# Attention steps placed between the products of the plain projections, in one hybrid trunk layer

## What is computed

```python
z = x @ w_in
# A: 16 heads of 64, 4 kv heads, window 128: a block of 128 queries sees its own and the previous 128 keys
s = einsum("bnqhgd,bnkhd->bnhgqk", q, k) * (dh ** -0.5) + bias
m = maximum(s.max(-1), sink)
p = exp(s - m)
A = einsum("bnhgqk,bnkhd->bnqhgd", p / (p.sum(-1) + exp(sink - m)), v)
# B: RWKV-7 time mixing, a scan over the tokens
mix = (sigmoid(gate_attn) * (A @ w_branch_attn) + sigmoid(gate_rwkv) * (B @ w_branch_rwkv)) @ w_out
h = layer_norm(alpha * x + mix)
# PEER: for each token and 8 heads, the 16 best of 128^2 experts
y = layer_norm(alpha * h + sum(gate * gelu(u[e] . h) * v[e]))
```

## Time and profile before

| | us |
|---|---|
| median of three runs | 4366.49 |
| lowest, highest | 4365.15, 4375.88 |
| the profiled execution | 4375.91 |
| its span on the core | 4374.1 |
| PE busy | 3791.0 (87%) |
| PE weight load busy (beside PE) | 2533.3 (58%) |
| DVE busy | 3035.9 (69%) |
| ACT busy | 958.0 (22%) |
| POOL busy | 1802.3 (41%) |

### The profile page before, as it was taken

How to read it: one execution, slowest core, us unless ns; L and a number is a source line. 1 busy time by engine, 2 the same in 40 slices (tenths; PEclk the granted TensorE clock), 3 DMA queues, 4 the chain that set the end, 5 groups by cost and what they waited for, 6 DMA issues and landing times. The chain is left out here.

```text
span 4374.1 us, 71420 instructions
## 1 busy us (share of the span) xinstructions
PE 3791.0 (87%) x28135; PEld 2533.3 (58%) x28135; DVE 3035.9 (69%) x5964; ACT 958.0 (22%) x2001; POOL 1802.3 (41%) x1489
## 2 busy tenths in 40 slices
PE   7976878799999888888778886668999999999998
PEld 6766765655555488787565464564544544455444
DVE  0454431678588658777777488876989788977777
ACT  1331230110133322222451013780000000000001
POOL 0007000057223034433225207735666566666665
PEclk9997879899999998898789997669999999999999
DMA  7542254389577467766549633459999999999998
GB/s 176 164 157 92 83 187 171 112 338 410 210 261 255 175 232 240 259 221 211 207 137 382 242 144 49 97 147 404 406 411 390 403 403 409 379 410 413 413 412 325
DMA packets 390906, 1152.47 MB, mean 263 GB/s; under 512 B 78174, under 2 KB 148387, under 8 KB 372995
## 3 DMA queue, kind: packets, MB, share of 16 engines
q0 software_dynamic: 207216, 687.87, 43.2%
q1 hardware_dynamic: 150628, 419.97, 25.9%
q10 hardware_dynamic: 32727, 40.05, 2.6%
HBM read 1044.67 MB, written 113.65 MB: 265 GB/s over the span
## 5 line engine op out<-in xcount | busy, mean ns | idle before, releaser
L2793 PE MATMUL x_vps<-l_c_v,x_w 128*128 128x512 f32 x1536 | 676.6, 602 | 38.4 <-DVE x_w L2842 38.4
L2785 PE MATMUL x_sps<-c_big,l_c_wo 128*128 128x384 f32 x2048 | 671.8, 490 | 26.8 <-DMA l_c_wo<-u_cols 23.6
L387 POOL DMA_INDIRECT l_w_ring<-u_rows,k_eidx x256 | 297.5, 1162 | 908.4 <-DVE l_w_dots L443 366.8
L387 POOL DMA_INDIRECT w_ring<-u_rows,k_eidx x384 | 478.2, 1245 | 402.2 <-DVE w_dots L443 238.5
L2785 PEld LDWEIGHTS x_sps<-c_big,l_c_wo 128*128 128x128 f32 x2048 | 391.5, 192 | 307.6 <-DMA l_c_wo<-u_cols 31.7
L460 DVE SCALAR_TENSOR_TENSOR l_c_share<-w_ring,w_wts,l_c_share 128x1024 f32<-128x1024 f32 x384 | 493.6, 1285 | 93.8 <-DMA w_ring<-v_rows,k_eidx 81.6
L2793 PEld LDWEIGHTS x_vps<-l_c_v,x_w 128*128 128x128 f32 x1536 | 296.4, 193 | 412.7 <-issue 361.4
L387 POOL DMA_INDIRECT w_ring<-v_rows,k_eidx x384 | 411.6, 1072 | 159.3 <-issue 109.6
L387 POOL DMA_INDIRECT l_w_ring<-v_rows,k_eidx x256 | 289.8, 1132 | 328.8 <-DVE l_w_yacc L460 264.8
L460 DVE SCALAR_TENSOR_TENSOR l_w_yacc<-l_w_ring,l_w_wts,l_w_yacc 128x1024 f32<-128x1024 f32 x256 | 328.9, 1285 | 28.0 <-DMA l_w_ring<-v_rows,k_eidx 19.4
L443 DVE CUSTOM_DVE_ANT_0 w_ring<-w_ring,w_h 128x1024 f32<-128x1024 f32 x256 | 302.9, 1224 | 38.4 <-DMA w_ring<-u_rows,k_eidx 26.2
(11 more groups left out here) (652 smaller groups left out, 6282.3 us busy)
## 6 DMA issues: line engine op xcount, KB each, us to landing
l_c_wo<-u_cols SPq DMA_DIRECT2D x64, 1024.0 KB, 9.4
l_c_v<-v_rows SPq DMA_DIRECT2D x32, 2048.0 KB
e_c_w<-w_tiles SPq DMA_DIRECT2D x54, 512.0 KB, 3.6
l_c_w<-w_tiles SPq DMA_DIRECT2D x54, 512.0 KB, 6.8
l_c_wo<-s_G SPq DMA_DIRECT2D x16, 1536.0 KB, 9.2
s_rw<-l_q_out SPq DMA_DIRECT2D x48, 384.0 KB, 5.2
s_G<-l_c_share ACTq DMA_DIRECT2D x8, 2048.0 KB, 7.9
s_zT<-l_pz ACTq DMA_DIRECT2D x30, 384.0 KB, 7.1
```

Of the source, the lines that this page charges most:

```text
L387: pool.indirect_dma_start(out=self.ring[:, r, :], out_offset=None, in_=self.A[table], in_offset=bass.IndirectOffsetOnAxis(ap=idx[:, s:s + ...
L2785: mm = pe.matmul(sps[n % 2][:, 0:ND * P], u[n % 4][:, k, :], hT[:, k, :], start=(k == 0), stop=(k == KT - 1))
L2793: mm = pe.matmul(vps[k][:, x * 512:(x + 1) * 512], w[:, e, k * P:(k + 1) * P], v[:, e, x * 512:(x + 1) * 512], start=(c == 0 and e == 0), ...
```

## The change

project_plain and attend become one stage, project_attend. After the first tiles alone (16 in e, 14 in l), the steps of attention and the remaining products share 10 (e) or 26 (l) slots. In a slot PE makes the scores of step s, the transposes of step s-1, one product of a column group, the values of step s-1, the output transpose of step s-2 and, in 4 (e) or 6 (l) of the slots, a second product. ACT makes the copy of step s-1, the exponentials of step s, and only then the eviction of the product. DVE makes the front of step s, shares of rows, the scaling of step s-1, and again shares of rows. In l, 14 groups of rows stand in the slots (slots 6 and 19 take two, each other one) and 10 before them: tiles 3 to 12 take one each; before, 19 stood in this stage and 6 in attention; the pairs, the scan and the merge keep their numbers.

Scores have one PSUM tile where there were two, products one bank for each column group. The operands of attention (keys, values, bias, two q blocks) are loaded from zT and s_tab by SP at tile 14, ahead of tile 15 in the queue, once the stores of tiles 0 to 11 have landed; sinks and penalties at the start. begin_act (the exponential of the first block's gates) moves from tile 5 to tile 2. The values are turned before the first slot, on PE and ACT. The attention output goes to a new DRAM scratch, aT, two tiles at a time on ACT's queue.

In part e the decode columns are no longer turned: ACT's queue stores the 128 x 8 columns to zn with a rearranged access pattern of single floats, one store per tile.

The scan works in the tile that the merge reads as bT, so that pairs 6 and 7 need no store and reload; in the last turn SP loads the first merge weights, the attention output, the first gates and the tiles 0 to 4 of bT, and tile 5 after the last chain. The merge begins with weights and gates in place, and side.clear is issued there, ahead of the loads of tile 1. The functions attend_tiles, kept_floats and load_attend go.

```diff
+def attend_loads(sp, A, pt, held, kv_in, att_in):
+    lo, at = (0, WIN) if pt.first else (pt.t0 - WIN, 0)
+    for name, t in (("kT", T_K), ("vT", T_V)):
+        sp.dma_start(held[name][:, :, at:], A["zT"][t:t + 2, :, lo:pt.t0 + pt.n].rearrange("t p c -> p t c")).then_inc(kv_in, 16)
+    src = bass.AP(A["tab"].tensor, WIN - 1, [[3 * WIN - 1, P], [P * 3 * WIN, NH], [1, 2 * WIN]])
+    sp.dma_start(held["bias"][:, :, :], src).then_inc(att_in, 16)
...
+    U0 = LAST_Q + (4 if pt.first else 2)
+    left = [(u, g) for u in range(U0, N_PLAIN) for g in range(NG)]
+    more = len(left) - SLOTS_
+    assert 0 <= more <= SLOTS_
+    mid_of, end_of, o = [], [], 0
+    for s in range(SLOTS_):
+        mid_of.append(left[o:o + 1])
+        e = (s + 1) * more // SLOTS_ - s * more // SLOTS_
+        end_of.append(left[o + 1:o + 1 + e])
+        o += 1 + e
...
+        zp = [psum(f"pzp{j}", [P, 512]) for j in range(2)]
+        scp, ptp = psum("a_scp", [P, UN, 2 * WIN]), psum("a_ptp", [P, UN, 2, WIN])
+        outp, atp = psum("a_outp", [P, 1, UN * HD]), psum("a_atp", [P, 1, 2, WIN])
...
+            sp.dma_start(sinks[:, :], A["sinks"]).then_inc(sink_in, 16)
+            sp.dma_start(pen[:, :], A["pen"]).then_inc(sink_in, 16)
+            blocks, rows_of = NBUF, 0
             for u in range(3, N_PLAIN + 2):
                 load(u)
-                if u < N_PLAIN:
+                if u == LAST_Q + 2:
+                    for j in range(2):
+                        sp.wait_ge(z_out[j], PER_Z * (LAST_Q // 2))
+                    if pt.first:
+                        sp.wait_ge(tab_out, 16)
+                    attend_loads(sp, A, pt, held, kv_in, att_in)
+                    for j in range(NBUF):
+                        load_q(j)
+                if u < U0:
                     bg.sp(sp, plan["groups"](u))
+                elif u < N_PLAIN:
+                    share = slot_groups * (u + 1 - U0) // (N_PLAIN - U0)
+                    bg.sp(sp, share - rows_of)
+                    rows_of = share
+                    while blocks < NBL and (u - U0 - 1) * NG >= (blocks - 1) * UNITS * len(left) // SLOTS_:
+                        sp.wait_ge(pe_done, PE.after(f"sc{UNITS * (blocks - NBUF + 1) - 1}"))
+                        load_q(blocks)
+                        blocks += 1
...
+            for s in range(SLOTS_):
+                if s < STEPS_:
+                    j, u = s // UNITS, s % UNITS
+                    if u == 0:
+                        pe.wait_ge(q_in[j % NBUF], 16 * (j // NBUF + 1))
+                    if s == 0:
+                        pe.wait_ge(pre_dve, N_PRE)
+                        pe.wait_ge(pre_act, N_PRE_ACT)
+                    else:
+                        pe.wait_ge(dve_done, DV.after(f"s2_{s - 1}"))
+                    for x in range(UN):
+                        t, h = 2 * u + x % 2, x // 2
+                        o = slice(h * HD, (h + 1) * HD)
+                        mm = pe.matmul(scp[:, x, :], q[j % NBUF][o, t, :], kT[o, u // 2, j * WIN:(j + 2) * WIN], start=True, stop=True)
+                    mm.then_inc(pe_done, 1)
+                m = s - 1
+                if 0 <= m < STEPS_:
+                    pe.wait_ge(act_done, AC.after(f"e{UN - 1}_{m}"))
+                    if m:
+                        pe.wait_ge(act_done, AC.after(f"cp{m - 1}"))
+                    for x in range(UN):
+                        for b in range(2):
+                            mm = pe.transpose(ptp[:, x, b, :], Sx[m % 2][:, x, b * WIN:(b + 1) * WIN], ident[:, :])
+                    mm.then_inc(pe_done, 1)
+                for u, g in mid_of[s]:
+                    unit(u, g)
+                if 0 <= m < STEPS_:
+                    j, u = m // UNITS, m % UNITS
+                    pe.wait_ge(act_done, AC.after(f"cp{m}"))
+                    if m >= 1:
+                        pe.wait_ge(dve_done, DV.after(f"on{m - 1}"))
+                    for x in range(UN):
+                        kv = 2 * (u // 2) + x // 2
+                        c = 2 * (x % 2) + x // 2
+                        for b in range(2):
+                            mm = pe.matmul(outp[:, 0, c * HD:(c + 1) * HD], PTs[m % 2][:, x, b, :],
+                                           vnat[:, j + b, kv * HD:(kv + 1) * HD], start=(b == 0), stop=(b == 1))
+                    mm.then_inc(pe_done, 1)
+                m = s - 2
+                if m >= 0:
+                    pe.wait_ge(dve_done, DV.after(f"on{m}"))
+                    if m >= 1:
+                        pe.wait_ge(act_done, AC.after(f"ac{m - 1}"))
+                    for x in range(2):
+                        mm = pe.transpose(atp[:, 0, x, :], on[m % 2][:, x * P:(x + 1) * P], ident[:, :])
+                    mm.then_inc(pe_done, 1)
+                for u, g in end_of[s]:
+                    unit(u, g)
...
+                if pt.dec:
+                    act.dma_start(A["zn"][:, u, :].rearrange("b p -> p b"), z[j][:, n:N], allow_slow_non_contiguous=True).then_inc(z_out[j], 16)
+
+            for u in range(U0):
+                for g in range(NG):
+                    evacuate(u, g)
+                if u == 2:
                     bg.begin_act(act)
                 bg.act(act, plan["groups"](u))
...
+            for s in range(SLOTS_):
+                m = s - 1
+                if 0 <= m < STEPS_:
+                    act.wait_ge(pe_done, PE.after(f"pt{m}"))
+                    if m >= 2:
+                        act.wait_ge(pe_done, PE.after(f"pv{m - 2}"))
+                    act.activation(PTs[m % 2][:, :, :, :], ptp[:, :, :, :], ACT.Copy).then_inc(act_done, 1)
+                if s < STEPS_:
+                    act.wait_ge(dve_done, DV.after(f"sd{s}"))
+                    for x in range(UN):
+                        act.activation(Sx[s % 2][:, x, :], Sx[s % 2][:, x, :], ACT.Exp, bias=nm[:, s, x:x + 1],
+                                       scale=HD ** -0.5, accum_out=sums[:, s, x:x + 1]).then_inc(act_done, 1)
+                    act.activation(es[:, s, :], sd[:, s, :], ACT.Exp).then_inc(act_done, 1)
+                for u, g in mid_of[s]:
+                    evacuate(u, g)
+                m = s - 2
+                if m >= 0:
+                    j, u = m // UNITS, m % UNITS
+                    act.wait_ge(pe_done, PE.after(f"at{m}"))
+                    if m >= 2:
+                        act.wait_ge(at_out[m % 2], 16 * (m // 2))
+                    act.activation(aTs[m % 2][:, :, :], atp[:, 0, :, :], ACT.Copy).then_inc(act_done, 1)
+                    act.wait_ge(act_done, AC.after(f"ac{m}"))
+                    there = slice(pt.t0 + j * WIN, pt.t0 + (j + 1) * WIN)
+                    act.dma_start(A["aT"][2 * u:2 * u + 2, :, there].rearrange("t p c -> p t c"), aTs[m % 2][:, :, :]).then_inc(at_out[m % 2], 16)
+                for u, g in end_of[s]:
+                    evacuate(u, g)
+                if sum(halves[:s + 1]) // 2 > sum(halves[:s]) // 2:
+                    bg.act(act, 1)
...
+            dve.wait_ge(sink_in, 32)
+            V.tensor_scalar(sink8[:, :], sinks[:, :], HD ** 0.5, None, ALU.mult).then_inc(pre_dve, 1)
+            dve.wait_ge(pre_dve, N_PRE)
             bg.begin_dve(dve)
-            bg.dve(dve, 8 * sum(plan["groups"](u) for u in range(N_PLAIN)))
+            bg.dve(dve, 8 * pre_groups)
...
+            for s in range(SLOTS_):
+                if s < STEPS_:
+                    j, u = s // UNITS, s % UNITS
+                    hs = slice(u * UN, (u + 1) * UN)
+                    if s == 0:
+                        dve.wait_ge(att_in, 16)
+                    dve.wait_ge(pe_done, PE.after(f"sc{s}"))
+                    if s >= 2:
+                        dve.wait_ge(pe_done, PE.after(f"pt{s - 2}"))
+                    do(f"s1_{s}", V.scalar_tensor_tensor(Sx[s % 2][:, :, 0:WIN], scp[:, :, 0:WIN], pen[:, pt.b0 + j:pt.b0 + j + 1],
+                                                         bias[:, hs, 0:WIN], ALU.add, ALU.add))
+                    do(f"s2_{s}", V.tensor_tensor(Sx[s % 2][:, :, WIN:], scp[:, :, WIN:], bias[:, hs, WIN:], ALU.add))
...
+                bg.dve(dve, 2 * halves[s])
+                m = s - 1
+                if 0 <= m < STEPS_:
+                    dve.wait_ge(act_done, AC.after(f"es{m}"))
...
+                bg.dve(dve, 2 * halves[s])
...
-        X, akT, an, Z, U, y0, y1, rk0 = (A["sb_big"][:, i * n:(i + 1) * n] for i in range(8))
+        X, akT, an, Z, rk0, U, y0, y1 = (A["sb_bT"][:, i, 0:n] for i in range(KT))
...
+            def load_merge(p):
+                first = A["sb_first"]
+                for x, name in enumerate(("wba_tiles", "wbr_tiles")):
+                    sp.dma_start(first["w"][x], A[name][0]).then_inc(merge_in, 16)
+                sp.dma_start(A["sb_aT"][:, :, 0:n], A["aT"][:, :, tokens].rearrange("t p c -> p t c")).then_inc(merge_in, 16)
+                for x, t in enumerate((T_GA, T_GB)):
+                    for here, there in pt.spans:
```

(37 more changed lines are left out.)

460 lines of the change are left out of this document (159 added, 301 removed).

## The result

The changed kernel is slower: 4449.1 us (median of 4 runs, 4436.2 to 4456.5) against 4371.2 us for the kernel before in the same session, a ratio of 1.0167 with a 95% interval of 1.0146 to 1.0188. Forecast was 4297 us.

| us from the stage's first product to the next one's | before | after | difference |
|---|---|---|---|
| e, plain projections (after: with attention) | 140.7 | 300.6 | +159.9 |
| e, pairs | 151.9 | 154.1 | +2.2 |
| e, scan (before: and attention) | 310.9 | 232.8 | -78.1 |
| e, merge | 78.8 | 92.6 | +13.8 |
| e, fronts | 143.7 | 142.4 | -1.3 |

A forecast was written before the change was run, and what follows sets the result against it. PE bounds l's plain projections and chains of short steps bound attention, so attention should hide beside projections. l -57 and e -12.5 make -69.5 us, 4297 us against the median of 4366.5; range 4262 to 4348.

The forecast's parts named there:

- Decode rows: e's projections: storing decode columns as single floats costs nothing; upper bound 50 ns a packet, +54 us.
- Rival C: e's projections: 4-byte stores take DMA time from tiles' stores and weights; about 4398 us at 75 ns a packet; chance 0.08.
- l's slots: l's projections with attention inside: 26 slots take 290 us, from 273 of PE work and 278 of DVE work.
- Rival A: Slots of l and e: the chain paces them, not PE or DVE; 1.2 us more each, about 4338 us; chance 0.22.
- The wait ahead of slot 0: l's projections: PE idle 10 us (5 to 20) while attention's operands, 4.8 MB, load.
- l as a whole: All of part l: projections +130, scan and attention -182, pairs and scan -5, together -57 us.
- the 3 us counted as saved elsewhere: l's projections: 3 us less outside the slots and the idle wait, included in the +130.
- The scan with attention: l: the 181 us attention stage goes, with some of the scan's tail; -182 us.
- The -5 for pairs and scan: l's pairs and scan: chooser parts leave the pairs' DVE, a wait for h falls where DVE has room; -5 us (0 to -12).
- 35 of slots and 12 of idle PE: e's projections with attention inside: +35 us for ten slots, 12 us idle at tile 15; +44 with a cold clock.
- Scan and attention: e: the old attention's 69 us go, less a hand-over of 1.5; -67.5 us.
- The merge cost: e's merge: second tile's weights queue behind the 8 MB zeroing, PE waits some 17 us; net +11 us (0 to +20).

The follow-up runs named there:

- zn_turned: Changed kernel with e's decode columns again turned by PE transpose, ACT copy and store by rows; ratio 0.9946 to the kernel before, e's projections 200.1 us.
- all_mended: Changed kernel, decode transpose restored but behind next slot's scores, bias loaded earlier, zeroing on POOL's queue, one more row group in l's pairs; ratio 0.992 to before.
- clear_in_fronts: As all_mended, but the 8 MB of zeros are sent on SP in e's fronts instead of POOL's queue; ratio 0.988 to before, 4317.9 us.

## Why the prediction was wrong

**The step that failed** is "Decode rows. I take nothing". It was worth about 97 us: 0.0221 of 4371 between the ratios of the changed kernel and zn_turned. I took the load of 1024 packets of 32 bytes as the nearest row and set 50 ns a packet as the upper bound, +54 us in all. Three things were wrong in that. The row was misread: the load landed in 4.9 us, and 1024/16 x 50 ns is 3.2 us, so the row lies above that product and not below it. It allows up to 77 ns a packet (4.9 us over 64) and does not speak against 50. Second, a single landing time says little of how many such transfers the engines take in a row. Third, the bound assumed that a packet has a price of its own, whatever its neighbours do, and that it leaves other transfers alone; the runs show 0.6 us a tile for floats 64 bytes apart and 3.1 us for the same floats side by side, and SP's loads at twice their time per megabyte. The true price lay outside my bounds, and the measured time outside my range.

The rule of the Trainium skill ("DMA: Bandwidth & Descriptors", Rules for kernel authors), that a strided last dimension lowers to one descriptor per element and that a transposing access pattern is far slower than other ways, pointed the right way. The packet price on the same page of the Trainium skill (section Bandwidth, about 10.5 ns) gives, as an estimate, 0.7 us of every engine per tile. The 8.7 ns a packet of the floats at 64 bytes agree with it, though the store was not hidden there either (0.6 us a tile); for the dense ones it is too low, and there the measurement decides.

**Rival C** named the mechanism, the place and the sign: the store in e's projections, ACT waiting for z stores, a period above 4.5 us. It gave 4398 us at 75 ns a packet; the measured time lies 51 us above. It had 0.08, too little: the only evidence against it was one row of another kind of transfer (a load, 32 bytes a packet), and that row, read rightly, does not make 50 ns too much. Its mechanism was the true one only in part: it priced the packets of the store, and left out that the transfers beside them slow down too.

**l's slots: right.** 290 us forecast, 287.5 measured, with PE 94% and DVE 91% busy. Rival A (the chain paces the slots) is refuted for l: PE waited 7.1 us for exponentials and 9.0 for DVE's s2 in all of its projections. For e it can only be judged without the single floats: in all_mended the slots take 86 us from the first scores to the end of the last product, as forecast. (The sum in A is 4297 + 43 = 4340, not 4338.)

**The wait ahead of slot 0: mis-sized.** 10 us forecast, 20 the upper bound, 24.7 measured (1.85 + 22.86). The mean DMA share of the stage hid a stretch that was full.

**l as a whole.** 130 forecast for the projections, 151.7 measured. Of the 21.7 between them, 14.7 are that wait; the turning of the values on PE, which had no term, is 2.0, the 28 halves ahead of it took 2.6 more than at 5.21 each, the change of stage 1.9 more, and the 3 us counted as saved elsewhere were not. The slots gave 2.5 back. The scan with attention: -179.7 against -182. The -5 for pairs and scan is not seen (-0.5 in the pairs, the scan inside its row). The merge's +6.9 was missed: "pairs, scan and merge keep their numbers" is true, but 24 groups ahead of the merge instead of 25 leave one more to its end, where DVE is last. Together l comes to -21.6 instead of -57.

**e.** The terms named for the projections, 35 of slots and 12 of idle PE, make 47 and more with a cold clock; the sum used 44. Scan and attention gave -78.1 instead of -67.5. The merge cost +13.8 against +11, by the mechanism named: PE waited 21.0 us at the second tile in the changed kernel. With the decode part turned again the projections stand at +59.4 instead of +44, of which 5.9 are six waits for ACT's copy that the placing of the transpose in that kernel brings. With the transpose elsewhere, the early bias and the rest, all_mended and clear_in_fronts stand at +44.6 and +46.5. So without the single floats the forecast of -70 comes out at -24 (0.0054 of 4371), and with the other edits at -52 (0.012).

**The signs.** The prediction named a sign for being wrong about the mechanism of the whole: the two attention stages' 245 us coming back as more than 190 in the two projection stages. They came back as 311.6 in the changed kernel, as 213.4 in zn_turned, and as 191.3 in clear_in_fronts. By that sign it fails even without the single floats: the attention work was hidden less well than I had set as the limit, by the loads ahead of slot 0 among others, until the other edits brought it near that limit. Of the other signs, the units' period above 4.5 us with evictions waiting for z stores pointed to C and was seen.

## What to carry to other kernels

A store of single elements cannot be priced by its packets or by its landing time: try it alone, because single floats side by side in DRAM slowed here both their own queue and SP's loads beside it. The zeroing of 8 MB cost 15 us wherever another transfer was waited for, on SP's queue and on POOL's, and nothing measurable in the fronts; put such a transfer where the share of the DMA engines is low. Read a row against a bound with both numbers written down: 4.9 us is not below 3.2. Before adding loads to a stage, cut its stretch finely: a mean share of 0.82 hid a stretch at 1.03.

## What was not expected of the hardware

The dependence on distance: 1024 single floats a tile cost 0.6, 0.8, 2.1 and 3.1 us at 64, 16, 8 and 4 bytes apart, at an equal number of packets (the first two not clearly apart). That side by side they double the time of loads on another queue. And the spread between chips in one stage above all: l's scan took 569 to 581 us on some and 603 to 608 on another, while l's plain projections of the same code took 465.2 to 465.9 and all that follows stood within 1%.
